# Stick-breaking heads: differences taken in V instead of in the weights, and the causal mask by GpSimd's affine select instead of mask matmuls

## The reference, cut to what matters

```python
z = jnp.einsum('bhqd,bhkd->bhqk', q[:, :, q0:q1], k[:, :, :q1]) * scale
strict = pos[:q1][None, :] < pos[q0:q1][:, None]
log_keep = jnp.where(strict, jax.nn.log_sigmoid(-z), 0.0)
log_rest = lax.cumsum(log_keep, axis=3, reverse=True) - log_keep
a = jnp.where(strict, jnp.exp(jax.nn.log_sigmoid(z) + log_rest), 0.0)
outs.append(jnp.einsum('bhqk,bhkd->bhqd', a, v[:, :, :q1]))
```

## Time and profile before

| what | us |
|---|---|
| median of 3 runs (lowest, highest) | 3178.75 (3178.54, 3179.42) |
| span of the profiled execution, first to last instruction | 3177.3 |
| PE busy / DVE busy / ACT busy / POOL busy | 3005.1 / 1491.1 / 724.1 / 355.3 |
| attention of layer 0, first score to last eviction of o | 318.9 to 441.6 |
| of it the stick-breaking groups, first scan to last subtract | 358.7 to 398.8 |
| attention of layer 1 starts at | 855.3 |

### The profile page before, as it was taken

How to read it: one execution, slowest core, us unless ns; L and a number is a source line. 1 busy time by engine, 2 the same in 40 slices (tenths; PEclk the granted TensorE clock), 3 DMA queues, 4 the chain that set the end, 5 groups by cost and what they waited for, 6 DMA issues and landing times.

```text
span 3177.3 us, 36092 instructions
## 1 busy us (share of the span) xinstructions
PE 3005.1 (95%) x14479; PEld 1659.0 (52%) x14479; DVE 1491.1 (47%) x2829; ACT 724.1 (23%) x1521; POOL 355.3 (11%) x218
## 2 busy tenths in 40 slices
PE   8999899998989899999999999999989887999998
PEld 5888443787744344446856533333345543444443
DVE  5994842998392434675575311211144753011112
ACT  1210542121262201111124201100015642111111
POOL 4553000655200000000001100000000000000000
PEclk9999999999999899999999899999999998999999
DMA  5452003456201222110412799999931003999997
GB/s 225 164 194 80 27 1 129 155 184 244 80 1 40 108 83 106 36 53 8 169 67 88 314 389 399 376 389 377 396 122 56 24 3 148 412 421 421 421 421 295
DMA packets 89896, 606.07 MB, mean 191 GB/s; under 512 B 10809, under 2 KB 11612, under 8 KB 19205
## 3 DMA queue, kind: packets, MB, share of 16 engines
q1 hardware_dynamic: 79776, 575.70, 45.4%
q0 software_dynamic: 4432, 15.73, 1.6%
q10 hardware_dynamic: 5524, 12.35, 1.2%
HBM read 592.73 MB, written 11.01 MB: 190 GB/s over the span
## 4 chain that ended last, share of the span: by engine, by line
PE 63%; DVE 7%; ACT 2%; issue 1%; another core or an unknown queue 0%; DVEq 0%; ACTq 0%; PEldq 0%
PE ps L1359 8%; PE ps L2763 7%; PE ps L2725 7%; PE ps L2776 4%; PE ps L2742 4%; PE ps L2806 4%; PE ps L1092 3%; PE ps L3056 2%; PE ps L2613 2%; PE ps L1457 2%; PE ps L2815 2%; PE ps L2529 2%; PE ps L2630 2%; PE ps L1697 2%; PE ps L3217 1%; PE ps L1509 1%
## 5 line engine op out<-in xcount | busy, mean ns | idle before, releaser
L611 PE MATMUL ps<-mem 128*128 128x256 f32 x1792 | 393.3, 381 | 13.2 <-DVE mem L641 10.8
L611 PEld LDWEIGHTS ps<-mem 128*128 128x128 f32 x1792 | 340.3, 191 | 65.5 <-DVE mem L641 14.4
L556 POOL TENSOR_TENSOR mem<-mem 128x512 f32<-128x512 f32 (+1 forms) x160 | 301.7, 1885 | 535.2 <-DVE mem L852 276.5
L754 DVE SCALAR_TENSOR_TENSOR mem<-mem 128x1024 f32<-128x1024 f32 x160 | 254.7, 1632 | 13.8 <-DMA mem<-in_ada_w 12.9
L1359 PE MATMUL ps<-mem 128*128 128x512 f32 (+1 forms) x768 | 254.7, 494 | 2.9 <-ACT mem L1200 2.9
L2763 PE MATMUL ps<-mem 128*64 128x512 f32 x1024 | 223.3, 594 | 0.0
L2725 PE MATMUL ps<-mem 128*64 128x512 f32 x1024 | 222.5, 592 | 0.7 <-ACT mem L2659 0.7
L1359 PEld LDWEIGHTS ps<-mem 128*128 128x128 f32 x768 | 147.5, 193 | 109.5 <-issue 98.3
L641 DVE TENSOR_TENSOR mem<-ps,mem 128x256 f32<-128x256 f32 x308 | 121.3, 418 | 111.9 <-PE ps L611 68.4
L1092 PE MATMUL ps<-mem 128*128 128x512 f32 x384 | 169.6, 597 | 1.8 <-DVEq L156 1.8
L2915 DVE TENSOR_TENSOR mem<-ps,mem 128x512 f32<-128x512 f32 x16 | 11.1, 691 | 314.1 <-PE ps L2725 314.1
(11 more groups left out here) (420 smaller groups left out, 4156.9 us busy)
## 6 DMA issues: line engine op xcount, KB each, us to landing
mem<-in_moe_w SPq DMA_DIRECT2D x384, 1024.0 KB, 13.9
mem<-in_w_in SPq DMA_DIRECT2D x48, 1024.0 KB, 8.1
mem<-in_ada_w SPq DMA_DIRECT2D x48, 1024.0 KB, 5.0
mem<-in_hy_w_in SPq DMA_DIRECT2D x24, 1024.0 KB, 6.9
mem<-in_w_out SPq DMA_DIRECT2D x12, 1024.0 KB, 6.0
mem<-in_k_win_l SPq DMA_DIRECT2D x8, 1024.0 KB, 6.9
mem<-in_hy_w_out SPq DMA_DIRECT2D x8, 1024.0 KB, 5.0
mem<-in_sw_w_in SPq DMA_DIRECT2D x6, 1024.0 KB, 7.1
```

Of the source, the lines that this page charges most:

```text
L556: gp(out, x, y, op).then_inc(A.mark(sem), 1)
L611: m = mm(seven(l, unit), x[:, k, :], y[:, k, :], start=(k == 0), stop=(k == 3))
L754: stt(PRODUCT if again else w, w, 1.0, C_ROWS[:, z, :], ALU.mult, ALU.mult, accum_out=mod(layer, b // KD, b % KD, z))\
```

## The change

For the stick-breaking heads the sum over keys of (C[k+1] - C[k]) V[k] is rewritten as the sum of (C[k] - 1)(V[k-1] - V[k]), with V[-1] = 0. So the subtraction is done once on V in the projection, and the weights that are transposed are C itself; the eviction subtracts 1 as it copies.

- In the projection: POOL zeroes the first row of `V_BEFORE` (which lies in `KT[:, 8:12]`, free until block 36) ahead of block 24's sums. ACT, ahead of block 30's copy, issues two DMAs from SBUF to SBUF that shift V by one row (1 MB and 6 KB). POOL, ahead of block 36's sums, waits for them and makes four differences of 128 x 512. ACT waits for those differences ahead of block 36's copy, which overwrites `V_BEFORE`.
- In the attention phase, kind 1: no mask matmul; after the sigmoid POOL sets the masked part of the diagonal tile (128 x 2 x 128) to 1 by an affine select; DVE's scan waits for that; DVE's subtract is gone; ACT's eviction is Identity with a bias of -1 in place of Copy. The ones in `P_SETS` are not set any more.
- Four new semaphore names share four that these phases do not use.

```diff
...
               "aux_full", "aux_act", "aux_dve", "sel_scaled", "pair_map", "ctx_map", "product", "inverted", "spread", "selected"]
+
+
+SHARED_SEMS = {"sums_made": "ctx_full", "v_moved": "ctx_out", "v_stepped": "ctx_turned", "masked": "ctx_silu"}
...
                 sems[n] = ctx.enter_context(nc.semaphore(f"{n}_{turn}"))
-            nums = [x.num for x in sems.values()]
+            for n, other in SHARED_SEMS.items():
+                sems[n] = sems[other]
+            nums = sorted({x.num for x in sems.values()})
             assert max(nums) - min(nums) == len(nums) - 1
...
             nc.vector.memset(MISC[:, 2:3], 0.0).then_inc(A.mark(), 1)
+            nc.vector.memset(MISC[:, 3:4], -1.0).then_inc(A.mark(), 1)
             for i, sem in enumerate(X_IN):
...
             for j in BLOCKS:
+                if j == 24:
+                    nc.gpsimd.memset(V_BEFORE[0:1, 0, :], 0.0).then_inc(A.mark("v_moved"), 1)
+                if j == 36:
+                    A.e.wait_ge(S["v_moved"], 33)
+                    for i in range(NQ):
+                        made(VN[:, NQ + i, :], V_BEFORE[:, i, :], VN[:, NQ + i, :], ALU.subtract, "v_stepped")
                 n, t = l * N_HYB + j // 4 * 2, j % 4
...
                     act(v(VN_ + 8 * 512, WCH), v(VN_ + 8 * 512, WCH), ACT.Silu).then_inc(A.mark("m_ready"), 1)
+                if j == 30:
+                    A.e.wait_ge(S["product_read"], READ_NO[24, 6, 1])
+                    e.dma_start(V_BEFORE[1:P], VN[0:P - 1, NQ:2 * NQ, :]).then_inc(S["v_moved"], 16)
+                    e.dma_start(V_BEFORE[0:1, 1:NQ, :], VN[P - 1:P, NQ:2 * NQ - 1, :]).then_inc(S["v_moved"], 16)
+                if j == 36:
+                    A.e.wait_ge(S["v_stepped"], NQ)
                 if j in BLOCKS:
...
         RT = v(GT_ + 11 * 512, 512)
+        V_BEFORE = KT[:, 8:12, :]
...
                         r = 64 * c
-                        mm(ps[:, b0 + c, 0:kw], QT[r:r + 64, tile, i * P:kw], KT[r:r + 64, tile, 0:kw], start=True, stop=False)
+                        m = mm(ps[:, b0 + c, 0:kw], QT[r:r + 64, tile, i * P:kw], KT[r:r + 64, tile, 0:kw], start=True, stop=kind == 1)
                     if kind == 2:
                         for c in range(2):
                             mm(ps[:, b0 + c, 0:kw], HOTS[0:72, 2 * pair + c, :], BIAS[0:72, 0:kw], start=False, stop=False)
-                    for c in range(2):
+                    for c in range(0 if kind == 1 else 2):
                         m = mm(ps[:, b0 + c, i * P:kw], IDB, MASK[:, kind, :], start=False, stop=True)
...
+        def pool_attn(A):
+
+            for s, (kind, pair, i) in enumerate(UN):
+                if kind == 1:
+                    A.e.wait_ge(S["probs"], s + 1)
+                    x = P_SETS[s % 4][:, :, 512 - P:512]
+                    nc.gpsimd.affine_select(x, x, [[0, 2], [-1, P]], ALU.is_gt, 1.0, base=0, channel_multiplier=1)\
+                        .then_inc(A.mark("masked"), 1)
+
         def act_attn(A):
...
                     src = ps[:, b:b + n, 0:(i + 1) * P].rearrange("p c (j q) -> p c j q", q=P)
-                    act(dst, src, ACT.Copy).then_inc(A.mark("turned_out"), 1)
+                    if kind == 1:
+                        act(dst, src, ACT.Identity, bias=MISC[:, 3:4]).then_inc(A.mark("turned_out"), 1)
+                    else:
+                        act(dst, src, ACT.Copy).then_inc(A.mark("turned_out"), 1)
                 if s < len(UN):
...
-            for pset in P_SETS:
-                nc.vector.memset(pset[:, :, 512:513], 1.0).then_inc(A.mark(), 1)
-            A.e.wait_ge(*A.last)
             for s in range(len(UN) + LAG + 1):
...
                     if kind == 1:
+                        A.e.wait_ge(S["masked"], u - 4 * NQ + 1)
                         for c in range(2):
                             keep = pset[:, c, 512 - kw:512][:, ::-1]
                             nc.vector.tensor_tensor_scan(keep, keep, one_col.to_broadcast([P, kw]), 1.0, ALU.mult, ALU.mult)\
-                                .then_inc(A.mark(), 1)
-                        A.e.wait_ge(*A.last)
-                        tt(pset[:, :, 512 - kw:512], pset[:, :, 513 - kw:513], pset[:, :, 512 - kw:512], ALU.subtract)\
-                            .then_inc(A.mark("weights"), 1)
+                                .then_inc(A.mark("weights" if c else None), 1)
                     else:
...
                     pool_hyb_proj(A, p // H_PHASES)
+                if p in (2, 2 + H_PHASES):
+                    pool_attn(A)
                 if p == PHASES_TO_SWA - 3:
...
```

## The result

The changed kernel takes 3257.61 us (median, 3257.27 to 3259.68) against 3179.09 of the kernel before beside it: a ratio of 1.0248, 95% interval 1.0236 to 1.026. That is 78.5 us slower, where 3177.0 was forecast with 3191 as the far end.

The account below looks back on a forecast made before the run. PE, busy 95% of the span, bounds the kernel, but DVE bounds the stick-breaking groups. Attention's gain and the move's cost gave 3178.75 - 5.0 + 3.2 = 3177.0 us, range 3169 to 3191.

Parts of the forecast that it names:

- The move: Projection, the 1 MB shift of V: 1.2 us in layer 0, 2.0 in layer 1, together 3.2, between 0 and 5.
- The differences and ACT's wait: Projection, POOL's four differences ahead of block 36, 5 to 9 us, and ACT's wait: nothing, 0.8 per layer at the slow end.
- Two DMA issues at 0.45 each: Projection, ACT ahead of block 30's copy: 0.9 us per layer, costed at nothing, 0.9 per layer if DVE stood waiting.
- the weight slot and then the load behind it: Projection: the move delays block 32's weight slot by 1.2 us in layer 0 and DVE's load in layer 1 by 2.0.
- the first rival: Attention, kind 1: select does not hold DVE or is short; group at 8.6 us, kernel 3172.2, or 3169; chance 0.30.
- The floor worked out step by step: Attention, kind 1: four steps of transpose, eviction, transpose over one pair of PSUM banks; 8.6 us per group whatever DVE does.
- the select and what it holds: Attention, POOL's select takes 0.726 us, upper end 1.265, and holds DVE 0.61 per select, 2.44 per group.
- a sign of being wrong: Attention, kind 1: the prediction is wrong if selects take over 1 us or the scans do not stretch.
- 8 x 0.63 = 5.0: Attention: each of eight groups goes from 9.83 to 9.2 us, 0.63 less, 5.0 us gained in all.
- The group in which the pipeline fills: Attention: the first group gains less, the crossing into kind 2 more, where ACT waits 1.13 us; the two cancel.
- Select long: Attention, kind 1 scans: a select of 1.265 us makes the group 11.0 us and the kernel 3191.3; chance 0.22.
- Paid back in the projection: Projection: full move (5), DMA issues uncovered (0.9 per layer), POOL's lead gone (0.8 per layer): 3182.2; inside the forecast's 0.48.

Follow-up runs that it names:

- 112 and 15: The changed kernel with its move of 127 partitions cut into transfers of 112 and 15, at the same place: 3184.96 us, ratio 1.002 to the kernel before.
- the early move: Against the kernel with 112 and 15: both transfers issued right behind ACT's copy for block 28 instead of ahead of block 30's; 3179.12 us, ratio 0.9997.
- the plain copy: Against the kernel with move and differences both early: kind 1's eviction is ACT.Copy instead of Identity with a bias column; measured once, 3170.93 us.
- the eviction's chain was cut in two: Against the kernel with select and move and differences early: in kind 1 ACT evicts, and PE awaits, each head's bank separately; 3171.36 us, ratio 0.9975.

## Why the prediction was wrong

**The move, the step that failed.** "At that rate it takes 2.5 us of all engines", between 0 and 5 in both layers. The step took for granted that a transfer of 1 MB goes over all DMA engines, because the loads of 128 partitions in the earlier trace rows do. None of those rows has 127 partitions, and 127 rows went over one engine: 26 GB/s, a landing after 60 and 70 us. The runs with 126, 122 and 112 rows show the count as the cause: nothing else differs between them and the changed kernel but one transfer more, which with 122 rows brought far less; and 72 to 74 us of the 78.5 go with 126 and 112. The Trainium skill states the rule (DMA: Bandwidth & Descriptors, section Why a DMA increments its semaphore by 16 and not by 1): the engines used are the largest number up to 16 that divides the slowest dimension of both sides, and 127 partitions get one. The runs agree for 127 (share 0.06), 122 (0.13) and 112 (0.97 where no load ran); for 126 they show only a rate above that of two engines. The prediction did not weigh this rule.

**The differences and ACT's wait.** "I cost it at nothing" and "finds the differences done one block earlier" were priced with the values in place at 233.45. With the landing at 273.85 POOL stood 25.59 us, ACT 11.48 for the differences, PE for both. The cover was there, and it was shorter than the wait.

**Two DMA issues at 0.45 each.** The move's took 1.24, and the second 21.58 as it stood behind the first. At the same place each took 0.55 to 1.43 with 126, 122 or 112 rows. With the 6 KB row first nothing stood, and nothing was gained, as POOL, ACT and PE then waited the longer for the landing.

**The size of the move when it is spread.** With 112 and 15 the projections cost 12.4 us (1.0020 - 0.9981), differences included, and the early move, which meets DMA engines that are mostly idle, takes 7.3 of them away. By the medians that is above the bound of 5; the two intervals leave some 4 us either way, so it is not shown to be. The kind of loss was forecast, the weight slot and then the load behind it, and both were mis-sized: POOL's wait for the slot grew by 16.59 - 13.93 = 2.66, where 1.2 was taken, and DVE's wait at 752, forecast to grow by 2.0, grew by 7.42 - 3.27 = 4.15.

**Attention: the first rival was right.** The forecast had a group of 9.2 us, the rival 8.6. Measured, from select to select, against the 9.83 of the earlier trace rows:

```profile
408.39:417.09 8.70, 8.26 (x54) 4.37 (x52) 6.81 (x9) 5.44 (x9) 2.05 (x5) 1.00 0.00 0
```

The floor worked out step by step was right to 0.1 us: transposes wait for ACT's eviction, and the bias column costs its 0.09 in three of the steps (the plain copy took 0.28 off the group). The mis-sized terms are the select and what it holds. The groups of scans and selects by line, then two selects and the scans beside them in the timeline:

```profile
L1082 DVE TENSOR_TENSOR_SCAN mem<-mem 128x128 f32<-128x128 f32 (+3 forms) x64 | 50.3, 834 | 16.3 <-POOL mem L1012 16.3
...
L1012 POOL TENSOR_SCALAR_AFFINE_SELECT mem<-mem 128x256 f32<-128x256 f32 x32 | 16.4, 512 | 159.6 <-ACT mem L1041 159.6
```

```profile
408.90 0.96 DVE L1082 TENSOR_TENSOR_SCAN mem<-mem 128x384 f32<-128x384 f32 x1 [1.16 <-POOL mem L1012]
...
409.67 0.41 POOL L1012 TENSOR_SCALAR_AFFINE_SELECT mem<-mem 128x256 f32<-128x256 f32 x1 [0.87 <-ACT mem L1041]
...
409.78 1.11 DVE L1082 TENSOR_TENSOR_SCAN mem<-mem 128x384 f32<-128x384 f32 x1
...
411.93 1.19 DVE L1082 TENSOR_TENSOR_SCAN mem<-mem 128x512 f32<-128x512 f32 x1
...
412.50 0.82 POOL L1012 TENSOR_SCALAR_AFFINE_SELECT mem<-mem 128x256 f32<-128x256 f32 x1 [2.42 <-ACT mem L1041]
```

A select took 0.51 us in the mean, not 0.726. All scans together grew from 49.0 to 50.3 us, 1.3 / 32 = 0.04 per select instead of 0.61. So the scans did not stretch, which the prediction had named as a sign of being wrong. Where the two engines meet, either can lose: the select at 412.50, which begins within a scan, took 0.82 us in place of 0.41, and the scan at 409.78, which begins within a select, took 1.11 where the one ahead of it, of the same size, took 0.96. The Trainium skill's rule on the shared ports (SBUF — State Buffer, section SBUF: two separate sides), which the prediction gave, lets whichever instruction begins first hold them to its end. The rows fit it only roughly: the select at 409.67 also begins within a scan, 0.19 us before the end of the one at 408.90, and lost nothing. No run tests the rule here. The 0.61 per select that the prediction took from the product's rows did not come. The select's price is DVE's waiting for it, 16.3 us in all. Except at the first scan this is hidden, since the group hangs on ACT and PE: DVE is busy for 6.81 of 8.70 us.

**The sum of attention.** "8 x 0.63 = 5.0" was nearly the measured 6.0, and that is luck: a steady group gains 1.13, not 0.63, but from first to last scan a layer gains only 3.7, three such steps and a little, and 0.7 goes to the first scan's wait: 3.0 per layer. The group in which the pipeline fills was taken to cancel against the crossing into kind 2, and did not.

**The rivals.** "Select long" (11.0 us a group) is out. "Paid back in the projection" named the right stage and had the wrong price: its dearest case was 8.4 us, the loss 87.2.

## What to carry to other kernels

Before a transfer is priced at the bandwidth of its neighbours, look at its row count: a shift by one row leaves 127 of 128, and here one row more or less was 74 us. A stall that stands out in a trace (an issue of 21.58 us) is not the cause until its removal moves the time; here what waited behind it would have waited anyway. And an operation taken from an engine that is not the bound of its loop need not show: leaving out the mask matmuls gained nothing that the times could tell, and the group fell to PE's own 8.05 us when the eviction's chain was cut in two.

## What was unexpected of the hardware

A transfer of 127 partitions within SBUF moved 26 GB/s and one of 122 moved 53, at DMA shares of 0.06 and 0.13, and ACT's next issue stood 21.58 and 23.96 us behind the first kind and under a microsecond behind the second. The affine select on 128 x 256 took 0.41 us undisturbed and up to 1.08 beside scans, where the two-input operation of as many elements takes 0.726. The granted clock in kind 2's stretch was 1.00 in some layers and executions and 0.93 to 0.96 in others, with the same instructions, which cost 1.6 to 2.7 us; what sets it, the runs do not show.
